# A mixture-of-experts decoder step: slots of an expert block handed to ranks in a permuted order

## The reference, cut to what matters

```python
lg = (h2 @ rg_w).astype(jnp.float32) + rg_b.astype(jnp.float32)
_, gsel = lax.top_k(lg, 1)
le_g = jnp.take_along_axis(le, gsel[:, :, None], axis=1)[:, 0]
ev, ei = lax.top_k(le_g, TOP_K)
eid = gsel * EXPERTS_PER_GROUP + ei
...
for e in range(N_EXPERTS):
    he = jax.nn.silu(h2 @ w_gate[e]) * (h2 @ w_up[e])
    out = out + combine[:, e:e + 1] * (he @ w_down[e])
```

## Time and profile before

| | |
|---|---|
| median of 3 runs | 1052.87 us (1051.36 to 1053.02) |
| the profiled execution | 1050.83 us |
| its span, first to last instruction | 1049.1 us |
| PE, PEld busy | 956.2 us (91%), 827.1 us (79%) |
| DVE, ACT busy | 691.9 us (66%), 491.9 us (47%) |
| POOL busy | 151.0 us (14%) |
| granted TensorE clock, mean | 0.974 |
| HBM read, written | 205.33 MB, 51.01 MB |

### The profile page before, as it was taken

One profiled execution on the slowest core, in us unless ns is written; L12 is line 12 of the kernel. 1 busy time (PEld: TensorE's weight loads), 2 busy tenths in 40 slices (PEclk: granted clock), 3 DMA queues, 4 the chain that ended last, 5 costly groups with the idle time before them and its releaser, 6 DMA issues.

```text
span 1049.1 us, 14773 instructions
## 1 busy us (share of the span) xinstructions
PE 956.2 (91%) x5420; PEld 827.1 (79%) x5420; DVE 691.9 (66%) x1041; ACT 491.9 (47%) x863; POOL 151.0 (14%) x146
## 2 busy tenths in 40 slices
PE   5999999989999999999999988999899899899850
PEld 4889999989999999998888765777666667676630
DVE  7457767796535535466566575897887787787834
ACT  7487785433223223233232232665556555655515
POOL 2000000000000000000300040454233233223120
PEclk9999999999999999999999998999999999999985
DMA  7114667336744754566323289999998999989308
GB/s 241 43 43 127 160 159 194 107 101 178 208 119 131 185 134 117 150 208 217 118 99 121 85 312 362 411 371 377 368 366 340 354 363 349 357 324 351 140 30 328
DMA packets 122922, 229.46 MB, mean 219 GB/s; under 512 B 71229, under 2 KB 84087, under 8 KB 114159
## 3 DMA queue, kind: packets, MB, share of 16 engines
q1 hardware_dynamic: 108102, 202.69, 57.1%
q0 software_dynamic: 14688, 25.79, 6.8%
q10 hardware_dynamic: 72, 0.20, 0.0%
HBM read 205.33 MB, written 51.01 MB: 244 GB/s over the span
## 4 chain that ended last, share of the span: by engine, by line
PE 66%; DMA 18%; DVE 8%; ACT 4%; issue 2%; SPq 0%; ACTq 0%; DVEq 0%; POOLq 0%
PE psum L1142 27%; DMA wd<-w_down 15%; PE psum L2057 10%; PE psum L2278 6%; PE psum L2351 4%; DMA wgu<-w_up 3%; PE psum L2282 2%; PE psum L1165 1%; PE psum L1992 1%; DVE wd_lo L2331 1%; ACT wd_hi L2327 1%; DVE it L954 1%; DVE xi L956 1%; ACT squares L2733 1%; PE psum L2263 1%
## 5 line engine op out<-in xcount | busy, mean ns | idle before, releaser
L1142 PE MATMUL psum<-hh,wh 128*128 128x350 f32 x672 | 223.4, 332 | 3.9 <-issue 3.9
L1142 PE MATMUL psum<-hh,wl 128*128 128x350 f32 x672 | 217.8, 324 | 0.0
L1142 PE MATMUL psum<-hl,wh 128*128 128x350 f32 x672 | 217.3, 323 | 0.0
L1142 PEld LDWEIGHTS psum<-hh,wh 128*128 128x128 f32 x672 | 127.7, 190 | 5.3 <-issue 4.1
L1142 PEld LDWEIGHTS psum<-hl,wh 128*128 128x128 f32 x672 | 127.4, 190 | 0.9
L1142 PEld LDWEIGHTS psum<-hh,wl 128*128 128x128 f32 x672 | 127.3, 189 | 0.0
L2254 DVE TENSOR_TENSOR wgu_lo<-wgu,wgu_hi 128x1536 fp32r<-128x1536 f32 x64 | 112.0, 1751 | 8.3 <-ACT wgu_hi L2249 8.1
L2331 DVE TENSOR_TENSOR wd_lo<-wd,wd_hi 128x2048 fp32r<-128x2048 f32 x32 | 73.3, 2292 | 59.2 <-ACT wd_hi L2327 58.8
L2249 ACT ACTIVATE wgu_hi<-wgu 128x1536 fp32r<-128x1536 f32 x64 | 94.9, 1484 | 25.6 <-DMA wgu<-w_up 25.2
L2327 ACT ACTIVATE wd_hi<-wd 128x2048 fp32r<-128x2048 f32 x32 | 61.3, 1916 | 70.4 <-DMA wd<-w_down 70.4
L2278 PE MATMUL psum<-wgu_hi,xgt_hi 128*128 128x512 f32 x192 | 92.6, 482 | 0.0
(11 more groups left out here) (340 smaller groups left out, 1828.0 us busy)
## 6 DMA issues: line engine op xcount, KB each, us to landing
wgu<-w_gate SPq DMA_DIRECT2D x34, 1024.0 KB, 8.5
wgu<-w_up SPq DMA_DIRECT2D x34, 1024.0 KB, 27.7
wd<-w_down SPq DMA_DIRECT2D x34, 1024.0 KB, 29.9
wst<-w_in SPq DMA_DIRECT2D x28, 512.0 KB, 4.1
ck<-qkv_rows SPq DMA_DIRECT2D x9, 702.0 KB
qkv_rows<-acc SPq DMA_DIRECT2D x12, 520.0 KB, 6.2
xb<-x SPq DMA_DIRECT2D x8, 512.0 KB, 4.4
wo<-w_out SPq DMA_DIRECT2D x8, 512.0 KB, 7.0
```

The lines of the kernel that those rows point to most:

```text
L1142: ins = mm(ps[:, c, 0:ZC], w[:, kk, :], a[:, kk, c * ZC:(c + 1) * ZC], start=(kk == 0 and q == 0), stop=(kk == KD - 1 and q == 2))
```

## The change

The iota that wrote 0, 1, 2, ... 127 into `ic` becomes four, one for each quarter of 32 slots.

```diff
-        it(ic[:, :], pattern=[[1, C]], base=0, channel_multiplier=0, **kw)
+
+        for k in range(4):
+            it(ic[:, 32 * k:32 * k + 32], pattern=[[2, 8], [32, 4]], base=16 * (k % 2) + k // 2, channel_multiplier=0, **kw)
```

## The result

The changed kernel takes 1011.26 us (median of 4 runs, 1009.78 to 1014.18) against 1052.17 us for the one before (4 runs): a ratio of 0.9615, 95% interval 0.9589 to 0.964. That is 40.9 us faster. The forecast was 1021 us with a range from 1014 to 1041: the direction and the mechanism held, and the gain was larger than the range allowed.

The account below looks back on a forecast made before the run. Unequally loaded DMA engines were taken to bound the expert stage after 723 us: 36.0 us of excess less 3.1 of waits and 1 for full blocks, net -32 from 1050.83 gives 1018.8, plus 2.04 to the median 1021 us; range 1014 to 1041.

Parts of the forecast that it names:

- Part 5: After the last expert block: only the last scatter changes, 0 to -0.5 us; clock dips 0 to -2 us; both taken as 0.
- Part 3: Row transfers in the expert stage: each half carries half the row time, 0.915 per engine, so 10.15 us a block.
- Imbalance among DMA engines as the bound: Main case, chance 0.73: in the expert stage from 723 us, engines serving the low 64 slots are overfull; balancing nets -32 us.
- fraction f = 0.77: Expert stage: share of row-transfer time on the half of the engines serving the low slots, giving loads 1.02 and 0.81.
- Part 1: Slot-table setup on POOL: one iota becomes four, three more costing 0.3 to 0.45 us, hidden in a gap, cost 0.
- Part 2: Slot-table values change but not shape: DVE comparisons and TensorE products keep their size, cost 0, TensorE's step stays 9.76 us.
- Part 4: Expert-stage weight loads: a 7.9 us lead lasts 20 steps, 8 wait 3.1 us; less 1 us for full blocks, net -32 us.
- The 36.0 us to be gained: Expert stage's second regime: 23 steps at 11.33 us instead of TensorE's 9.76, the whole excess available there.
- half relief: Rival, chance 0.12: packets slow in the upper half or stalls remain, 10.5 to 11 us a block, 1041 us.
- the memory as a total limit: Rival, chance 0.07 counted with queues averaging out imbalance: memory sets a total rate, balance moves nothing, 1052.9 us.
- the other map: Rival, chance 0.08: slots go to engines in turn, so the new order overloads half of them, 12.3 us a block, 1076 us.
- lower case: Low end of the main case's range, 1014 us: all 36 us of waits and 2 us of clock regained.

Follow-up runs that it names:

- four orders: Slot orders new, 32-slot pieces, old and every second group of four, each with a quarter less TensorE work: 9.78, 10.59, 11.30 and 11.42 us a step.
- the two full kernels with 8.0 rows: Against the kernel before: every second group of four slots filled first, 1057.11 us; new order with the lowest eight ranks on one engine, 1063.88 us.
- the two orders with like halves: Against the kernel before: ranks placed in 32-slot pieces alternating between halves, 1023.16 us; every second group of four slots filled first, 1057.11 us.
- the relieved kernel: Changed kernel's slot order, low-part products and most of their subtractions left out in most blocks, against the kernel before: 999.59 us, ratio 0.9508.
- the one-engine run: New slot order, but the lowest eight ranks fill one engine's eight slots in every block, against the kernel before: 1063.88 us, ratio 1.0104.
- pieces of 32: Ranks 32 to 63 moved to slots 64 to 95, ranks 64 to 95 to slots 32 to 63, against the kernel before: 1023.16 us; relieved of low-part products, 1023.61.
- that of the old one: Old slot order with low-part products and most of their subtractions left out in most blocks, against the kernel before: 1054.23 us, ratio 1.0025.

## Why the prediction was right, and where it was not

The direction and the mechanism were right, the size was not. Two terms of the sum failed. The larger is Part 5, the end, put at 0: it gave 5.1 us, because the step after the last turn had waited too. The other is Part 3, the balanced pace, put at 10.15 us: it is 9.78, so the 4 us of waits and full blocks that Parts 3 and 4 left over were not there. The rest of the miss is scatter between executions, as worked out below.

- *Imbalance among DMA engines as the bound* was right, and is shown: one engine filled by design undoes the gain, and the pace follows the fullest engine over four orders. The map that the prediction took from the Trainium skill, "DMA: Bandwidth & Descriptors", section "The descriptor swizzle", is given there for a full transfer of 128 partitions. The counts by it put the pace of all nine runs in the right order, save the 0.17 us between the two full kernels with 8.0 rows, for indirect transfers with skipped slots; the map by eights in a row does not.
- *Halves and engines.* The sum itself went by halves: each half with half of the row time, so 0.915 "for every engine". That doesn't follow, as the two orders with like halves show (34 us apart). It did no harm because the chosen order levels the single engines as well, 3.6 to 4.5 rows each by the count. The fraction f = 0.77 of the row time on the lower half was near: 53.7 of 64.6 rows lie there in the old order, 0.83.
- *Part 1, the iotas*: four took 0.64 us instead of 0.24, hidden, as forecast. *Part 2*: TensorE's step stayed at 9.76 us. Both right.
- *Part 3, the balanced pace*: right in kind, wrong in size. It was taken as 10.15 us with bounds 9.7 and 10.4; the relieved kernel measures 9.78. The term came from the mean share of 0.915 over the old order, read as load. Part of it was not load: 9.78 us at a share of 1.02 is 9.98 us of engine time a block, and 11.33 x 0.915 had given 10.37. So the same work had 4% more record time in the old order. That its packets stretched on engines with slack is the likely reading, from the one-engine run, and is not shown by itself. The lower bound, by the 412 GB/s of the earlier trace rows (9.7 us), was the better reading, since that window had all engines busy. I had chosen the longer window for its length, when its mean of 392 GB/s already held dips.
- *Part 4, the lead*: there is one, but its amount was too small. 7.9 us counted only the five steps from 674.69 us. With pieces of 32 the loads need 10.59 us a block, and TensorE still ran 18 steps at 9.76: an estimated lead of 18 x 0.83 = 15 us, in a run whose expert stage also began 5 us later (659.45 against 654.33 us). At 9.78 us hardly any lead was needed. So neither the 3.1 us of waits nor the 1 us for full blocks appeared. The 36.0 us to be gained were 35.3: I had counted to the last of eight transposes at one end and from the first at the other.
- *Part 5, the end*: taken as 0 with bounds that add to 2.5 us; measured 5.1. This is the largest single miss. The wait in the step after the last turn (14.0 us against 9.76) was in the rows and I did not count it; the gaps further on gave 0.6 (a wait of TensorE, 4.64 to 4.02) and the last scatter 0.2 (2.60 to 2.37).
- Altogether the forecast for a profiled execution, 1018.8, was missed by 6.6 us: 3.3 in the steps (35.3 less 32) and 5.1 at the end, less 1.7 of unrelated work before and 0.1 between span and time. The other 3.0 us to the median of 1011.26 are chance: the profiled execution of before lay 2.04 us under its median, the one of after 0.97 us over it.
- *The rivals*: half relief, the memory as a total limit and the other map are all refuted. The first would need stretched packets with full engines, and the relieved kernel moves 413 GB/s for 225 us. The Trainium skill, "DMA: Bandwidth & Descriptors", section "Where 436 GB/s comes from", states about 358 GB/s for a core as what binds between HBM and SBUF. The 413 GB/s go against it: here, with one core at work, the measurement decides.
- *The range* ended at 1014 because its lower case gave all waits back but nothing of the 24th step, and because no case held a median below its profiled execution.

## What to carry to other kernels

Where DMA engines set the pace, as here, the fullest one does. For an indirect transfer with skipped rows, count the filled partitions for each engine, not the partitions touched: groups of four, with their partners 32 above, belonged together in these runs. Queues that were never empty at a share below full meant imbalance here; but how much a balance will give is read from a stretch in which all engines are full, not from the mean share. And when a bound goes, its waits go in every step that had one, those after the last turn included.

## What the runs showed that I had not expected

- The mean DMA share is 0.91 both with half of the engines overfull and with one of sixteen. With the one, the records hold 49 us of engine time for each MB of rows, against 44 in the old order and 42 in the new one.
- The balanced pace of the DMA engines (9.78 us) and TensorE's (9.76) meet within 0.02 us. Relieving TensorE alone gained nothing in these steps, and 12 us before them. A kernel that relieves only the DMA engines was not run.
- POOL's issue of the gather (L2102) and of the scatter (L2210) got longer, as the page of the changed kernel shows:

```profile
L2210 POOL DMA_INDIRECT sum_rows<-total,slot_rows x34 | 71.1, 2092 | 31.7 <-DVE total L2365 22.6
...
L2102 POOL DMA_INDIRECT xg<-h_rows,slot_rows x34 | 62.7, 1844 | 25.4 <-DVE slot_rows L1917 10.5
```

Before, the scatter took 1668 ns and the gather 1200 ns on average, and 1662 and 1149 ns with one full engine, whose rows are spread over the partitions too. The gather goes with the pace in every order: 1606 ns with the pieces of 32, 1927 in the relieved kernel of the new order, 1108 in that of the old one. The scatter does not in the relieved kernels: it takes 1308 ns in the new order and 1222 in the old. What lengthens them was not tried.
